# Squares added in pairs ahead of four more means in a two-block transformer kernel

## The reference, cut to what matters

```
def rms_norm(x, w):
    y = x * lax.rsqrt(jnp.mean(x * x, axis=-1, keepdims=True) + EPS)
    return y * w

h = rms_norm(x, norm_w) * (1 + scale) + shift     # for the tokens, and for the context
p = h @ w_in                                       # 256 + 384 + 256 + 64 columns
q_lat  = rms_norm(p[..., :384], qa_w)              # after the first 256 columns
kv_lat = rms_norm(p[..., 384:640], kva_w)
k_pe   = rms_norm(p[..., 640:], kn_w[128:])
q  = q_lat @ w_qb
kv = kv_lat @ w_kvb
```

## Time and profile before

| what | value |
|---|---|
| time, median of 3 runs | 2271.38 us (2269.86 to 2274.02) |
| profiled execution | 2269.67 us |
| its span, first to last instruction | 2267.7 us |
| mean granted TensorE clock | 0.995 |
| TensorE busy | 2211.0 us (98%) |
| VectorE busy | 1177.3 us (52%) |
| ScalarE busy | 879.2 us (39%) |
| GpSimd busy | 932.8 us (41%) |

### The profile page before, as it was taken

How to read it: one execution, slowest core, us unless ns; L and a number is a source line. 1 busy time by engine, 2 the same in 40 slices (tenths; PEclk the granted TensorE clock), 3 DMA queues, 4 the chain that set the end, 5 groups by cost and what they waited for, 6 DMA issues and landing times.

```text
span 2267.7 us, 36911 instructions
## 1 busy us (share of the span) xinstructions
PE 2211.0 (98%) x13959; PEld 1900.5 (84%) x13959; DVE 1177.3 (52%) x1926; ACT 879.2 (39%) x1532; POOL 932.8 (41%) x767
## 2 busy tenths in 40 slices
PE   6999999999999999999999999999999999999998
PEld 4878979888888888889899988888888887788777
DVE  5785781657777763435244365553234115761273
ACT  5434353341111113325455442222444236742572
POOL 2435443343334443334353155555665441154323
PEclk9999999999999999999999999999999999999999
DMA  7242241125555541111211035553223332123212
GB/s 279 81 150 75 72 161 63 56 94 195 194 192 175 196 149 65 65 63 67 71 48 34 10 102 186 185 196 109 94 96 105 94 101 75 50 84 102 71 48 75
DMA packets 67720, 245.40 MB, mean 108 GB/s; under 512 B 7376, under 2 KB 11728, under 8 KB 66960
## 3 DMA queue, kind: packets, MB, share of 16 engines
q1 hardware_dynamic: 67360, 242.94, 31.3%
q0 software_dynamic: 240, 0.79, 0.1%
HBM read 240.81 MB, written 2.10 MB: 107 GB/s over the span
## 4 chain that ended last, share of the span: by engine, by line
PE 76%; issue 3%; DVE 2%; ACT 2%; POOL 1%; POOLq 0%; DVEq 0%; ACTq 0%
PE ps L888 14%; PE ps L889 14%; PE ps L890 14%; PE ps L1780 4%; PE ps L1783 4%; PE ps L1782 4%; PE ps L2010 2%; PE ps L1996 2%; PE ps L1948 1%; PE ps L925 1%; PE ps L926 1%; PE ps L927 1%; PE ps L637 1%; PE ps L2027 1%; POOL w_low L490 1%
## 5 line engine op out<-in xcount | busy, mean ns | idle before, releaser
L490 POOL TENSOR_TENSOR w_low<-ring,w_high 128x512 fp32r<-128x512 f32 (+2 forms) x534 | 746.0, 1418 | 1030.5 <-ACT w_high L481 1023.8
L481 ACT ACTIVATE w_high<-ring 128x1024 fp32r<-128x1024 f32 (+2 forms) x267 | 275.2, 1032 | 918.8 <-PE ps L890 623.7
L888 PE MATMUL ps<-h_high,w_high 128*128 128x512 f32 x1040 | 407.7, 392 | 4.4 <-DVE h_low L737 2.8
L889 PE MATMUL ps<-h_low,w_high 128*128 128x512 f32 x1040 | 405.9, 390 | 0.0
L890 PE MATMUL ps<-h_high,w_low 128*128 128x512 f32 x1040 | 405.4, 390 | 0.0
L888 PEld LDWEIGHTS ps<-h_high,w_high 128*128 128x128 f32 x1040 | 195.9, 188 | 47.9 <-issue 4.1
L890 PEld LDWEIGHTS ps<-h_high,w_low 128*128 128x128 f32 x1040 | 195.6, 188 | 41.4
L889 PEld LDWEIGHTS ps<-h_low,w_high 128*128 128x128 f32 x1040 | 195.9, 188 | 38.1
L3246 DVE TENSOR_TENSOR hidden<-arena,hidden 128x1536 fp32r<-128x1536 f32 (+1 forms) x42 | 87.2, 2076 | 193.3 <-ACT hidden L2363 193.3
L2913 DVE CUSTOM_DVE_ANT_0 const<-const,arena 128x1024 f32<-128x1024 f32 x96 | 154.9, 1629 | 56.5 <-DMA const<-late_w_dram 56.5
L1780 PE MATMUL ps<-hidden,w_high 128*128 128x512 f32 (+1 forms) x504 | 178.6, 354 | 0.0
(11 more groups left out here) (553 smaller groups left out, 4747.8 us busy)
## 6 DMA issues: line engine op xcount, KB each, us to landing
const<-late_w_dram SPq DMA_DIRECT2D x112, 512.0 KB, 5.0
ring<-up_dram SPq DMA_DIRECT2D x88, 512.0 KB, 3.3
ring<-down_dram SPq DMA_DIRECT2D x44, 512.0 KB, 3.2
XB<-ada_dram SPq DMA_DIRECT2D x22, 768.0 KB, 5.4
ring<-winE_dram SPq DMA_DIRECT2D x32, 512.0 KB, 3.5
ring<-win_dram SPq DMA_DIRECT2D x20, 512.0 KB, 3.2
ring<-winC_dram SPq DMA_DIRECT2D x20, 512.0 KB, 3.5
arena<-ada_dram SPq DMA_DIRECT2D x10, 768.0 KB, 19.7
```

The lines of the kernel that those rows point to most:

```text
L481: nc.scalar.activation(WH[p][:, 0:L], RAW[p][:, 0:L], ACT.Copy).then_inc(w_hi, 1)
L490: ins = nc.gpsimd.tensor_tensor(WL[p][:, to], RAW[p][:, to], WH[p][:, to].bitcast(F32), ALU.subtract)
L888: nc.tensor.matmul(bank[:, 0:n], wh[:, cols], hi, start=(k == 0), stop=False)
L889: nc.tensor.matmul(bank[:, 0:n], wh[:, cols], lo, start=False, stop=False)
```

## The change: pairs for four more items

`PAIRED` gets ("n2", 1), ("nlat", 0), ("nlat", 1) and ("nlat", 2). An odd last tile, as the query latent's third, stays alone. GpSimd gets the new adds at five places of its order: the context's ahead of the low parts of chunks 4 and 5, the query latent's between those of chunks 6 and 7, the two others after chunk 7; its loop over chunks 6 and 7 is written out. TensorE reads the odd tiles only, at the places where it read all of them.

```diff
-PAIRED = (("n2", 0), ("n4", 0))
+PAIRED = (("n2", 0), ("n2", 1), ("nlat", 0), ("nlat", 1), ("nlat", 2), ("n4", 0))
...
         def first_of_pair(stage, k, j):
-            return (stage, k) in PAIRED and j % 2 == 0
+            return (stage, k) in PAIRED and j % 2 == 0 and j + 1 < len(ITEMS[stage][k][0])
+
+        def second_of_pair(stage, k, j):
+            return (stage, k) in PAIRED and j % 2 == 1
 
         def pair_no(stage, k, j):
-            return KT // 2 * PAIRED.index((stage, k)) + j // 2
+            return sum(len(ITEMS[x][y][0]) // 2 for x, y in PAIRED[:PAIRED.index((stage, k))]) + j // 2
...
-            tiles_ = [KT - 2, KT - 1] if stage in LAST_APART else [KT - 1] if stage in ADDED else range(1, KT, 2) if (stage, k) in PAIRED else range(len(srcs))
+            tiles_ = [KT - 2, KT - 1] if stage in LAST_APART else [KT - 1] if stage in ADDED else [j for j in range(len(srcs)) if not first_of_pair(stage, k, j)]
...
-                    if (stage, k) in PAIRED:
+                    if second_of_pair(stage, k, j):
                         pe.wait_ge(sq_pair, pair_no(stage, k, j) + 1)
...
                 if c in (2, 3):
-                    mean(pe, "n2", 1, range(KT // 2 * (c - 2), KT // 2 * (c - 1)))
+                    mean(pe, "n2", 1, range(KT // 2 * (c - 2) + 1, KT // 2 * (c - 1), 2))
...
                 if c == 5:
-                    mean(pe, "nlat", 0, (0, 1))
+                    mean(pe, "nlat", 0, (1,))
...
                     if stage == "winM":
-                        first = 3
                         for k in range(4, 6):
+                            add_pairs("n2", 1, range(KT // 2 * (k - 4) + 1, KT // 2 * (k - 3), 2))
                             split_lo(stage, k)
                     if len(ITEMS[parted[stage]]) == 2:
                         odd_lows(parted[stage], 1)
+                    if stage == "winM":
+                        split_lo(stage, 6)
+                        add_pairs("nlat", 0, (1,))
+                        split_lo(stage, 7)
+                        for k in (1, 2):
+                            add_pairs("nlat", k, (1,))
...
+                if stage == "winM":
+                    continue
                 with pool.Fori(first, n // 2) as i:
```

## The result

The changed kernel took 2274.99 us (median of 20 runs, 2272.24 to 2280.7), the kernel before 2271.84 us beside it (20 runs, 2268.54 to 2276.12). The ratio is 1.0018 with a 95% interval of 1.0011 to 1.0025: slower by some 4 us, clear of noise, and outside the range of the forecast (2271.2 us, at most 2274.5). The waits came where they were forecast and as long as forecast. What the forecast gave too little weight is what they did to TensorE's clock.

What follows compares the result with a forecast made beforehand. TensorE, busy 98% of the span, was taken to bound the kernel. Terms +0.5 - 0.90 + 1.54 - 0.90 - 0.45 = -0.2 us, on the 2271.38 us median, gave 2271.2 us, range 2267.3 to 2274.5.

Steps and rivals of the forecast that it cites:

- the context's second block: Halved context block before chunk 4: sums ready before TensorE asks, saving 0.90 us.
- the two last items: Key and value latents for tokens and context: adds fit GpSimd's idle time, saving 0.90 and 0.45 us.
- The context's first block: Block before chunk 3: TensorE waits for adds queued behind that chunk's split, costing +0.5 us.
- a full block by VectorE: Context's first block: VectorE's line 851 could delay the second add by up to 0.49 us; left out of the sum.
- The query latent's block: Before chunk 6: add queued behind that chunk's split, TensorE waits 2.43 us, chunk 6 starts 1.54 us later.
- the sum: All blocks' gains and delays together, clock kept full: -0.2 us, bounds -0.75 to +0.75; chance 0.50.
- rival (a): Query latent's wait makes TensorE's clock fall, losing 1.4 us: +1.2 us in all, 2272.6 us; chance 0.30.
- The range: Whole kernel's time: from 2267.3 us to 2273.5, plus one for scatter, 2274.5 us.
- Within 0.2%: Whole kernel's time differs by less than 0.2% (4.5 us) from before; chance 0.87.
- Rival (b): All sums ready when TensorE asks, the query latent's too: 4.05 us saved, 2267.3 us; chance 0.10.

Runs made afterwards that it cites:

- e10: Changed kernel with useless matmuls filling both TensorE waits, five ahead of the context's first half and ten ahead of the query latent's pair; 1.0011 against the kernel before.
- e1: Kernel before with only the query latent's pair added, all other items summed singly; ratio 1.0038 against the kernel before.
- e9: Kernel before, no new pair, chunk 6 split in eight pieces and awaited by TensorE ahead of the query latent's mean; 1.0032 against the kernel before.
- e3: Changed kernel with ten useless 128x512 matmuls ahead of the query latent's mean, filling that wait; ratio 1.0020 against the kernel before.
- e11: The changed kernel run a second time, unaltered; ratio 1.0024 against the kernel before.
- e8: Changed kernel with chunk 6's split moved ahead, context's first half summed inside chunk 3, query latent's pair inside chunk 6; 0.9980 against the kernel before.
- e7: Changed kernel with GpSimd's split of chunk 6 moved ahead of the context's odd low parts; ratio 1.0007 against the kernel before.
- e4: Changed kernel with the mean of the query latent's pair moved from after chunk 5 to within chunk 6; 1.0012 against the kernel before.
- e5: Kernel before with only the context's pairs added, all latents summed singly; ratio 0.9997 against the kernel before.

## Why the prediction was wrong

**The savings and the waits were right.** Halved blocks gave -0.88 at the context's second block and -1.01 at the two last items (forecast -0.90 and -1.35). The missing 0.34 us is nearly all at the last one: behind its four records the first matmul of qb came after an idle time of 0.18 us that the profile puts down to issue. The context's first block cost +0.68 (+0.5 forecast); its two adds took 1.62 us, 0.14 more than alone. So of the 0.49 us that a full block by VectorE would have cost, the trace shows less than a third. The query latent's block cost +1.74 at full clock (e10; +1.54 forecast), the wait 2.34 us (2.43). At full clock the sum was +0.54 us where the forecast had -0.2, within its bounds of -0.75 to +0.75.

**The step that failed** is the clock behind the query latent's wait: the sum kept it at full, a loss of nothing, and the fall was left to rival (a) with a chance of 0.30. The forecast itself said of (a): "It decides if the wait is as long as forecast." The wait was as long as forecast, and the fall came with it, in both traces of the changed kernel and in those of e1 and e9; a clock below 1.00 in the stretch was the sign named for (a). The trace of before had two like blocks of short records, one with a fall and one without, and both without any idle time (a third, at 1149.63, was not followed by one either). The forecast took from them a chance below even for a stretch that is emptier, 2.3 us of nothing and then short records.

**Its price was mis-sized too.** Rival (a) took 1.4 us, from a fall of 3.4 us over matmuls of 256 columns. In the changed kernel the clock stayed low for 6.8 us: 12.51 - 10.11 = 2.40 us in chunk 6, and 12.62 - 11.88 = 0.74 us up to it, mostly for the 8 short records that themselves ran at half clock. That is 3.1 us. With it the sum is 0.54 + 3.1 = 3.7 us, what the trace shows and close to the runs' 4. For each us at half clock the forecast was nearly right (1.4 / 3.4 = 0.41, measured 3.1 / 6.8 = 0.46); its length was too short. That rate was partly luck: the row with 20 records holds a part of a block of short ones too. By the starts of 36 matmuls, 4.40 us at 1145.23 and 5.89 us at 1160.47 in the trace of before, that fall cost 1.5 us. Between executions the length differs: 3.4 us in e1.

**The range** ended at +0.75 + 1.4 + 1 us for that reason, and the median of 2274.99 lies 0.5 us beyond it. Nearly as much is the base, which is chance: the forecast took 2271.38, the median of three runs, and twenty gave 2271.84. "Within 0.2%" (0.87) came true at 0.18%, but not through the sum that carried most of that chance, and twenty runs do tell 0.18% from none, which the forecast doubted. Rival (b) is excluded by the wait in both traces.

**The runs outside the stretch.** With 0.46 us lost for each us at half clock, an estimate from the first trace, the cost at full clock and the extra time at half clock over all runs give 3.7 us for e3 (0.57 + 0.46 x 6.7), 7.3 for e1 (1.74 + 0.46 x 12.1), 6.7 for e9 (1.89 + 0.46 x 10.5), 4.8 for e11 and 1.5 for e10. The means of their runs lie 3.7, 7.4, 7.2, 5.3 and 1.8 us above those of the kernel before. So what e1, e3 and e9 lost beyond the stretches shown is time at half clock too. In which places of which executions it lies, and what part the wait has in it, stays open: falls elsewhere differ from one execution to the next, and a single trace can't count them.

## What to carry to other kernels

Price a new wait of a dense TensorE with what it does to the clock behind it: here 1.9 to 2.3 us of idle time next to short matmuls cost 7 to 8 us alone (e9, e1), and 4 to 5 net of what the halved blocks saved (the change). When work is moved to an engine that serves its queue in order, list what stands ahead of it in the queue and ask for its result one chunk later, inside work that doesn't need it; e8, which does that and moves the split of chunk 6 ahead in the queue, turned +0.18% into -0.2%.

## What was not expected of the hardware

The clock did not fall while TensorE waited, but when it had resumed, and then slowed the dense work that follows: in the changed kernel full clock during the idle 2 us, half for the next 6.8; in e7 and e9 the fall came some 1.2 us after TensorE had resumed. A wait of 0.92 us ahead of 0.9 us of one-column matmuls was followed by a fall (e7), and the context's wait, 0.96 and 0.23 us, by one in four of the seven traces in which it stood unfilled (e4, e5, e7 and e11). The Trainium skill's page "TensorE: Matmul & The Clock Gate", section "Why this matters for your kernels", warns of gaps longer than these; in this kernel shorter ones did it (2.34, 1.89 and 0.92 us), where the matmuls beside them had a single column. And the useless matmuls of e3 and e10 cost next to nothing that the wait had not cost already, and both traces show the clock full behind them; over all runs it is e10 that comes back near the kernel before (30.6 us at half clock against 28.5), e3 does not (34.7 against 28.0).
